# Retention queries and keys with features on the partitions, and a front with host-ordered transfers

## The chip, the cores and the metric

The kernel runs on one core of a Trainium2 chip. Its time is the device time of one execution in microseconds; the median of several runs counts, and beside it stands one profiled execution, from which all rows are taken.

## The reference, cut to what matters

A model of four layers over 256 latent tokens and 256 context tokens of 1024 features, in float32. The change touches the first layer, a retention mixer, and the way in which all weights are read. Cut to that:

```python
# modulation: silu(c) @ ada_w + ada_b -> shift, scale, ... (6 chunks of 1024)
def modulate(x, shift, scale):
    return rms_norm(x) * (1.0 + scale) + shift

# retention_mixer, 4 heads, q and k of 256, v of 512 features per head
q, k, v, g = split(h @ w_in)              # for latents and for context
k = k * RET_DK ** -0.5
ql, kl = rope_2d(ql), rope_2d(kl)         # only the latents are rotated
att = einsum('bihd,bjhd->bhij', q, k) * decay_mask
o = einsum('bhij,bjhv->bihv', att, v)     # latents see latents and context
y = (group_norm(o) * norm_g * silu(g)) @ w_out
```

`rope_2d` takes the 256 features of a head in two halves of 128, one by the token's row and one by its column; in each, feature i is rotated with feature i + 64.

## The kernel before

Everything is written out by hand, one instruction queue for each engine, with semaphores between them. Weights pass in units of 128 x 2048 floats (1 MB). SyncE's queue (SP) loads them in order of use into three raw slots, each unit with two transfers of 512 KB (L394), and waits for a slot until VectorE has made the low part of the unit that lay in it. ScalarE makes the high part of a unit (`w_hi`, a copy to the fp32r format, L609), VectorE the low part (`w_lo`, the difference, L1241). Activations are kept in two parts as well (`hT_hi`, `hT_lo`, cast L1371 and subtraction L1246; 8 k-tiles of 128 features x 512 tokens, of which 256 are latents and 256 context). A product is three matmuls: high by high, high by low, low by high (L2326, L2327, L2321 with the activations standing in the array; L2336, L2337, L2340 with the weights standing). `ahead(name)` on ScalarE and VectorE splits all units up to two behind the named one.

The front: `x` and `ctx` are normed (squares and root on ScalarE, product on VectorE, L1282), turned on TensorE (`x_turned`, L2269) and copied out of PSUM by ScalarE (L658). Meanwhile the modulation's first four chunks of 512 columns (2 MB each, in `FRONT_IN`) are multiplied on TensorE (`chunk`, `sums`, L2283), the sums copied as rows by VectorE (`row`, L1323), turned into columns (`to_cols`) and added up (`mod_cols`, L1331 and L1333). With shift and scale known for four k-tiles, ScalarE modulates (`modulate`, L630) and VectorE splits (`rows_split`). TensorE's queue takes latents and context apart: units `qa0` and `qb0` (queries and keys of head 0, k-tiles 0 to 3 and 4 to 7) are multiplied for token tiles 0 and 1 first, then for 2 and 3. The small vectors come as rows and are turned on TensorE (`cols_full`). `awake` multiplies zeros while TensorE would have nothing to do. The decay of the heads is a short series on VectorE (`decay_start`, `series`, `decay_end`), with one exponential on ScalarE between.

A head has six units: `qa`, `qb`, `g0`, `g1`, `va`, `vb`. `strip` makes queries and keys with tokens on the partitions; ScalarE copies them to `QK` (keys scaled, L705, L706), VectorE rotates (L1464 to L1468, semaphore `roped`), TensorE turns them with 16 transposes (L2269), ScalarE copies them to `QKT` (L720), and the score matmuls (L2457) read that. Between the transposes and the scores TensorE does the first k-tile of `vb`; behind the scores, the other three. VectorE multiplies the scores with the mask (L1487). Into the heads VectorE also weighs the later chunks of the modulation (`weigh`, L1361 and L1363), whose pieces of 1 MB GpSimd's queue (POOL) loads (L537), each as soon as the buffer is read. Head 0 begins on VectorE with the mask's arguments (L1433, L1434) after a wait for two transfers of constants; ScalarE's mask exponentials (L697 to L700) come ahead of its high part of `g00`.

Of the kernel before, what the change touches and what calls it, by code (L numbers as in the profile page):

```python
# [15 lines left out]
ALU = mybir.AluOpType  # L16
# [3 lines left out]
P = 128  # L20
# [29 lines left out]
C_ALL = C_MB + 768  # L50
# [62 lines left out]
FRONT = (0, 2, 1, 3)  # L113
# [66 lines left out]
def build(nc, A, out):  # L180
    ctx = ExitStack()
    with ctx:
        at_byte = [16512]

        def sb(name, shape, dt=F32, word=None):
            o = at_byte[0] if word is None else word
            n = 4 * math.prod(shape[1:])
            if word is None:
# [36 lines left out]
        names = ["unit_used", "hi_ready", "lo_ready", "out_stored", "const_in", "vec_in", "x_in", "x2_in", "dec_in",  # L225
# [3 lines left out]
                 "rstd_ready", "on_hi", "on_lo", "ident_in", "sz_set", "cols_full", "cols_read", "c_in",  # L229
                 "xt_full", "xt_read", "xm_ready", "h_part", "front_used", "xc_in", "ada_used", "row_ready", "at_full",  # L230
                 "mod_ready", "qk_read", "g_read", "qkt_full", "qkt_read", "sc_full", "sc_read", "v_read",
# [41 lines left out]
        vec, vec2, vec_c, lvec = at(8192, 128), at(8320, 128), at(8448, 128), const[:, C_DIST:C_DIST + 256]  # L273
# [51 lines left out]
        QK, PT, QKT, ON = at(0, 4, 512), at(0, 6, 256), at(2048, 4, 512), at(2048, 4, 512)  # L325
        VN, GT, ROPE = at(4096, 4, 512), at(6144, 4, 512), at(9728, 256)
# [55 lines left out]
        def _(sp):  # L382
            s = Side()

            def load(view, n, part):

                u = s.loaded
                assert n == SIZES[u], (u, n, SIZES[u])
                r = RAW_OF[u]
                v = RAW_BEFORE[u]  # L390
                if v is not None:
                    sp.wait_ge(sem["lo_ready"], v + 1)
                for j in range(2):
                    sp.dma_start(view(raw[:, r, 0:n], j), part(j)).then_inc(unit_in[r], 16)  # L394
                s.loaded += 1

            def by_k(w, k0, nk, c0, n):

                b = [0, nk // 2, nk]
                load(lambda d, j: d.rearrange("p (k n) -> p k n", k=nk)[:, b[j]:b[j + 1], :], nk * n,  # L400
                     lambda j: kpn(w)[:, k0 + b[j]:k0 + b[j + 1], c0:c0 + n])

            def pair(w, c0, gap):

                load(lambda d, j: d.rearrange("p (k g n) -> p k g n", k=KD, g=2)[:, :, j, :], UNIT,
                     lambda j: kpn(w)[:, :, c0 + j * gap:c0 + j * gap + P])

            def part(w, k0, c0, gap):

                load(lambda d, j: d.rearrange("p (k g n) -> p k g n", k=4, g=2)[:, :, j, :], UNIT,  # L410
                     lambda j: kpn(w)[:, k0:k0 + 4, c0 + j * gap:c0 + j * gap + 256])
# [2833 lines left out]
```

## Time and profile before

| | |
|---|---|
| median of 3 runs | 2022.6 us (2022.3 to 2022.95) |
| the profiled execution | span 2020.7 us, which is 1.9 us below that median |
| TensorE busy | 1988.9 us, 98% |
| VectorE, ScalarE, GpSimd busy | 1322.7, 857.5, 68.4 us |
| granted TensorE clock, mean | 0.997 |
| read from memory | 316.48 MB, 157 GB/s over the span |

The span runs from the first to the last instruction of the profiled execution. A busy engine is one that has an instruction in it; TensorE's are pipelined, so its true pace is the distance from one start to the next.

### The profile page before, as it was taken

The numbers are of one execution on the slowest core, as the hardware profiler recorded it, in microseconds if no ns is written. First come the engines' busy times: TensorE is split into PE (matmuls) and PEld (weight loads), VectorE is DVE, ScalarE is ACT, GpSimd is POOL, SyncE is SP. The second block draws the span as 40 slices with busy tenths as digits, with TensorE's granted clock in tenths as the row PEclk, the third lists the DMA queues.
The fourth block names the chain that finished last, engine by engine and source line by source line (L and its number), as shares of the span: only waits on it lengthen the run. The fifth ranks groups of instructions, "written<-read, shape, count | busy, mean of one in ns | idle before, by whom it ended". The sixth has DMA issues, their size and how long they took to land.

```text
span 2020.7 us, 25508 instructions
## 1 busy us (share of the span) xinstructions
PE 1988.9 (98%) x10263; PEld 1654.0 (82%) x10263; DVE 1322.7 (65%) x1642; ACT 857.5 (42%) x1007; POOL 68.4 (3%) x121
## 2 busy tenths in 40 slices
PE   8999999999999999999999999999999999999998
PEld 5878778778888888877778888899888888988887
DVE  5886979556555354576776565766866577678565
ACT  5332332224322222446665554554544356445442
POOL 0000000010111000000000000000000000000000
PEclk9999999999999999999999999999999999999999
DMA  9544444252554343332137555545655554546552
GB/s 357 184 151 136 144 148 145 84 167 74 172 155 158 104 151 126 102 113 84 53 103 219 168 177 177 188 165 170 216 194 193 176 172 162 196 157 218 189 190 81
DMA packets 250759, 319.19 MB, mean 158 GB/s; under 512 B 10113, under 2 KB 166066, under 8 KB 250130
## 3 DMA queue, kind: packets, MB, share of 16 engines
q1 hardware_dynamic: 235152, 262.77, 40.2%
q0 software_dynamic: 14416, 53.14, 7.8%
q8 instruction: 81, 1.33, 0.3%
q10 hardware_dynamic: 1074, 1.66, 0.2%
q14 instruction: 36, 0.29, 0.1%
HBM read 316.48 MB, written 1.05 MB: 157 GB/s over the span
## 4 chain that ended last, share of the span: by engine, by line
PE 86%; DVE 6%; ACT 2%; DVEq 2%; DMA 1%; issue 1%; ACTq 1%; SPq 0%
PE ps L2326 14%; PE ps L2327 14%; PE ps L2321 8%; PE ps L2881 6%; PE ps L3142 6%; PE ps L2340 5%; PE ps L2336 5%; PE ps L2337 5%; PE ps L2798 3%; PE ps L2269 3%; PE ps L3145 3%; PE ps L2406 2%; PE ps L2887 2%; PE ps L2891 2%; PE ps L2888 2%; PE ps L2801 2%
## 5 line engine op out<-in xcount | busy, mean ns | idle before, releaser
L1241 DVE TENSOR_TENSOR w_lo<-raw,w_hi 128x2048 fp32r<-128x2048 f32 (+1 forms) x244 | 553.0, 2271 | 239.1 <-ACT w_hi L609 238.3
L609 ACT ACTIVATE w_hi<-raw 128x2048 fp32r<-128x2048 f32 (+1 forms) x244 | 462.0, 1897 | 254.3 <-PE ps L2321 149.6
L2326 PE MATMUL ps<-w_hi,big_hi 128*128 128x512 f32 x760 | 298.8, 393 | 0.9 <-DVE big_lo L1739 0.7
L2327 PE MATMUL ps<-w_hi,big_lo 128*128 128x512 f32 x760 | 296.2, 390 | 0.0
L2336 PE MATMUL ps<-hT_hi,w_hi 128*128 128x512 f32 (+1 forms) x512 | 192.4, 380 | 1.9 <-issue 1.0
L2337 PE MATMUL ps<-hT_lo,w_hi 128*128 128x512 f32 (+1 forms) x512 | 190.3, 376 | 0.0
L2326 PE MATMUL ps<-w_hi,hT_hi 128*128 128x512 f32 x416 | 167.7, 403 | 4.6 <-DVE hT_lo L1246 4.6
L2326 PEld LDWEIGHTS ps<-w_hi,big_hi 128*128 128x128 f32 x760 | 142.8, 188 | 30.4 <-issue 1.0
L2327 PEld LDWEIGHTS ps<-w_hi,big_lo 128*128 128x128 f32 x760 | 142.9, 188 | 28.9 <-issue 0.5
L2327 PE MATMUL ps<-w_hi,hT_lo 128*128 128x512 f32 x416 | 163.2, 392 | 0.0
L3142 PE MATMUL ps<-h_both,w_hi 128*128 128x512 f32 x512 | 128.0, 392 | 0.0
L1363 DVE SCALAR_TENSOR_TENSOR raw<-front,const,raw 128x512 f32<-128x512 f32 x168 | 118.8, 748 | 7.0 <-issue 1.3
L2340 PE MATMUL ps<-hT_hi,w_lo 128*128 128x512 f32 (+1 forms) x512 | 119.8, 376 | 0.6 <-DVE w_lo L1241 0.6
L2326 PE MATMUL ps<-w_hi,h_both 128*128 128x512 f32 (+1 forms) x288 | 110.9, 388 | 3.2 <-DVE h_both L1246 3.2
L2336 PEld LDWEIGHTS ps<-hT_hi,w_hi 128*128 128x128 f32 x512 | 96.4, 188 | 20.3 <-issue 1.7
L2337 PEld LDWEIGHTS ps<-hT_lo,w_hi 128*128 128x128 f32 x512 | 96.5, 188 | 17.1 <-issue 0.2
L2327 PE MATMUL ps<-w_hi,h_both 128*128 128x512 f32 (+1 forms) x288 | 108.5, 380 | 0.0
L2321 PE MATMUL ps<-w_lo,big_hi 128*128 128x512 f32 x424 | 108.4, 390 | 0.0
L2321 PE MATMUL ps<-w_lo,hT_hi 128*128 128x512 f32 x416 | 108.2, 392 | 0.0
L2340 PEld LDWEIGHTS ps<-hT_hi,w_lo 128*128 128x128 f32 x512 | 92.3, 188 | 18.2 <-DVE w_lo L1241 0.8
L3142 PEld LDWEIGHTS ps<-h_both,w_hi 128*128 128x128 f32 x512 | 92.8, 189 | 17.1
L2326 PEld LDWEIGHTS ps<-w_hi,hT_hi 128*128 128x128 f32 x416 | 78.8, 189 | 25.7 <-issue 5.3
(314 smaller groups left out, 3027.4 us busy)
## 6 DMA issues: line engine op xcount, KB each, us to landing
raw<-ffn_w_in SPq DMA_DIRECT2D x88, 512.0 KB, 5.1
raw<-w_in SPq DMA_DIRECT2D x80, 512.0 KB, 4.6
raw<-w_up SPq DMA_DIRECT2D x64, 512.0 KB, 4.7
raw<-w_down SPq DMA_DIRECT2D x64, 512.0 KB, 4.5
raw<-ret_w_in SPq DMA_DIRECT2D x48, 512.0 KB, 5.4
front<-ada_w POOLq DMA_DIRECT2D x24, 1024.0 KB, 5.5
raw<-ffn_w_out SPq DMA_DIRECT2D x40, 512.0 KB, 4.5
raw<-ada_w POOLq DMA_DIRECT2D x64, 256.0 KB, 4.3
```

The lines of the kernel that those rows point to most:

```text
L609: act.activation(SPLIT_HI[PAIR_OF[u]][:, 0:m], raw[:, RAW_OF[u], 0:m], ACT.Copy).then_inc(sem["hi_ready"], 1)
L1241: op(SPLIT_LO[PAIR_OF[u]][:, 0:m], raw[:, RAW_OF[u], 0:m], SPLIT_HI[PAIR_OF[u]][:, 0:m].bitcast(F32), ALU.subtract).then_inc(sem["lo_ready ...
L1363: i = stt(out=acc[:, m, :], in0=rows[:, x, :], scalar=SZ[:, k, m:m + 1], in1=acc[:, m, :], op0=ALU.mult, op1=ALU.add)
L2269: return pe.transpose(out, src, ident[0:src.shape[0], 0:src.shape[0]])
L2321: i = pe.matmul(bank(b + t), x(k0 + k)[0][:, t * P:(t + 1) * P], w[1][:, k, :], start=False, stop=last and k == nk - 1)
L2326: pe.matmul(out, x[0][:, t * P:(t + 1) * P], w, start=start, stop=False)
L2327: pe.matmul(out, x[1][:, t * P:(t + 1) * P], w, start=False, stop=False)
L2336: pe.matmul(out, w[0][:, k, js], hT(k)[0][:, c:c + n], start=(k == 0), stop=False)
L2337: pe.matmul(out, w[0][:, k, js], hT(k)[1][:, c:c + n], start=False, stop=False)
L2340: i = pe.matmul(out, w[1][:, k, js], hT(k)[0][:, c:c + n], start=False, stop=(k == KD - 1))
L2881: i = pe.matmul(dst, x(k0 + k)[0][:, t * P:(t + 1) * P], w[1][:, k, :], start=False, stop=stop and k == nk - 1)
L3142: pe.matmul(out, w[0][:, k, js], h2_both[:, :, k, :], start=(k == 0), stop=False)
```

## The change

Queries and keys of all heads are made with features on the partitions: `features` takes the weights as the standing and the activations as the moving operand, as `feature` did for the gates. ScalarE copies the latents' queries and keys to `QKL` and those of the context straight to `QKT`. VectorE rotates the latents from `QKL` into `QKT`; the partner of a feature lies 64 partitions away, so the product with the sine is written across (`SWAP`). The 16 transposes, their PSUM copy and the semaphores `qkt_full` and `qkt_read` are gone; `roped` is now waited for behind the first k-tile of `vb`. The keys' scale is applied with the mask. The cosines and sines lie with features on the partitions; those of the column half are a third transfer of constants (`ROT_COS[1]`), queued on POOL behind `mod_ready` 4 and ahead of the pieces of the later modulation.

All weights come in one array in order of use, each unit with 8 KB in a row for each partition, in one transfer. The modulation's chunks are stored likewise; chunk j of the first four now holds 256 columns of shift and 256 of scale, so each serves two k-tiles. The small vectors come as columns, with no turning. `x` and `ctx` are loaded first, then `qa0`, chunks 0 to 2, `qb0`, chunk 3. In the front latents and context go together: `first_high` and `first_low` multiply one k-tile for all 512 tokens, as soon as VectorE has it (`modulated`, which takes ScalarE's part as well); ScalarE copies the rows instead of VectorE.

```diff
@@ SP
-                for j in range(2):
-                    sp.dma_start(view(raw[:, r, 0:n], j), part(j)).then_inc(unit_in[r], 16)
+                    sp.dma_start(raw[:, r, 0:m], A["units"][u, :, 0:m]).then_inc(unit_in[r], 16)
             def modulation(j):
+                for h in range(2):
+                    sp.dma_start(FRONT_IN[2 * j + h], A["ada"][j, :, 4 * h:4 * h + 4, :]).then_inc(front_in[2 * j + h], 16)
             sp.dma_start(X4[:, 0:2, :], token_rows(A["x"][0])).then_inc(sem["x_in"], 16)
+            sp.dma_start(X4[:, 2:4, :], token_rows(A["ctx"][0])).then_inc(sem["xc_in"], 16)
+            load(FIRST_END["qa0"])
             modulation(0)
+            modulation(1)
             modulation(2)
+            load(FIRST_END["qb0"])
             modulation(3)
+            load(TOTAL_UNITS)
@@ POOL
-            pool.wait_ge(front_in[3], 32)
-            fetch(X4[:, 2:4, :], token_rows(A["ctx"][0]), sem["xc_in"])
-            pool.wait_ge(sem["front_used"], 2)
+            pool.wait_ge(sem["front_used"], 1)
             fetch(dec[:, 0, :], bcast(A["ret_decay_logit"].rearrange("a b c -> a (b c)"), 8), sem["dec_in"])
...
             pool.wait_ge(sem["front_used"], 4)
             fetch(const[:, C_DIST:C_SZ], A["table"][:, C_DIST:C_SZ], sem["const_in"])
             fetch(const[:, C_RS:C_SEL], A["table"][:, C_RS:C_SEL], sem["const_in"])
+            pool.wait_ge(sem["mod_ready"], 4)
+            fetch(ROT_COS[1], A["table"][:, C_RK:C_RK + 256], sem["const_in"])
@@ ACT
+            first_squares(0)
+            first_root(0)
+            first_squares(1)
+            first_root(1)
+            for t in range(4):
+                turned_x(t)
             split(FIRST_END["qa0"])
+            row(0, 8960, 1)
+            row(1, 9472, 2)
             act.wait_ge(sem["dec_abs"], s.next("dec_abs"))
             act.activation(dec[:, 2, :], dec[:, 1, :], ACT.Exp, scale=-1.0).then_inc(sem["dec_exp"], 1)
+            row(0, 8960, 3)
             split(FIRST_END["qb0"])
+            row(1, 9472, 4)
...
-                    act.wait_ge(sem["const_in"], 32)
+                    act.wait_ge(sem["const_in"], 48)
...
-                act.activation(QK[:, :, 0:256], ps[:, a:a + 4, 0:256], ACT.Copy)
-                act.activation(QK[:, :, 256:512], ps[:, a:a + 4, 256:512], ACT.Copy, scale=RDK ** -0.5).then_inc(sem["qk_read"], 1)
+                act.activation(QKL, ps[:, a:a + 4, 0:256], ACT.Copy)
+                act.activation(QKT[:, :, 256:512], ps[:, a:a + 4, 256:512], ACT.Copy).then_inc(sem["qk_read"], 1)
...
-                act.wait_ge(sem["qkt_full"], h + 1)
-                act.activation(QKT[:, :, :], ps[:, b:b + 4, :], ACT.Copy).then_inc(sem["qkt_read"], 1)
@@ DVE
+            def modulated(c):
+                xm = at(4096 + 512 * c, 2, 256)
+                for m, x in enumerate((XTL, XTC)):
+                    ts(xm[:, m, :], x[:, c, :], mod[:, 0, 8 + c, m:m + 1], mod[:, 0, c, m:m + 1], ALU.mult, ALU.add)
+                drain()
+                dve.tensor_copy(hT_hi[:, c, :], at(4096 + 512 * c, 512))
+                drain()
+                lo(hT_lo[:, c, :], at(4096 + 512 * c, 512), hT_hi[:, c, :]).then_inc(sem["h_part"], 1)
+            first_norm(0)
+            first_norm(1)
+            dve.wait_ge(sem["xt_read"], 4)
+            mod_cols(2, 0)
+            modulated(0)
+            modulated(1)
             split(FIRST_END["qa0"])
+            mod_cols(3, 1)
+            modulated(2)
+            modulated(3)
@@
+            mod_cols(2, 2)
+            modulated(4)
+            modulated(5)
+            split(FIRST_END["qb0"])
             decay_start()
             series(15, 13, 11, 9)
+            mod_cols(3, 3)
+            modulated(6)
+            modulated(7)
             decay_end()
@@ DVE, in a head
+                for n in range(2):
+                    x = QKL.rearrange("p (g n) t -> p g n t", n=2)[:, :, n, :]
+                    y = QKT.rearrange("p (g n) t -> p g n t", n=2)[:, :, n, 0:256]
+                    sn = ROT_SIN[n].unsqueeze(1).to_broadcast([P, 2, 256])
+                    for r in (0, 64):
+                        op(SWAP[64 - r:P - r], x[r:r + 64], sn[r:r + 64], ALU.mult)
+                    op(y, x, ROT_COS[n].unsqueeze(1).to_broadcast([P, 2, 256]), ALU.mult)
+                    drain()
+                    i = op(y, y, SWAP, ALU.add)
...
-                    i = op(PT[:, t, :], sc[:, t, :], g, ALU.mult)
+                    i = stt(out=PT[:, t, :], in0=sc[:, t, :], scalar=RDK ** -0.5, in1=g, op0=ALU.mult, op1=ALU.mult)
@@ PE
+            pe.wait_ge(sem["ones_set"], 1)
+            awake(24)
+            pe.wait_ge(sem["ident_in"], 16)
             x_turned(0)
             x_turned(1)
+            awake(8)
             x_turned(2)
             x_turned(3)
+            pe.wait_ge(sem["silu_c"], 1)
+            chunk(0, 0)
+            awake(4)
+            to_cols(2, 8960)
+            awake(8)
+            first_high("qa0", 0)
+            first_high("qa0", 1)
+            chunk(1, 1)
+            first_low("qa0", 0)
+            to_cols(3, 9472)
+            first_low("qa0", 1)
             chunk(2, 0)
+            first_high("qa0", 2)
+            to_cols(2, 8960)
+            first_high("qa0", 3)
+            first_low("qa0", 2)
+            used(first_low("qa0", 3))
             chunk(3, 1)
+            first_high("qb0", 4)
             to_cols(3, 9472)
+            first_high("qb0", 5)
+            first_low("qb0", 4)
+            first_low("qb0", 5)
+            first_high("qb0", 6)
+            first_high("qb0", 7)
+            first_low("qb0", 6)
+            used(first_low("qb0", 7))
@@ PE, in a head
-                    used(strip(a, f"qa{h}", hT, 0, 4, range(4), True, False))
+                    used(features(a, f"qa{h}", 0, range(4), 0, 512, True))
...
+                strip(a, f"vb{h}", hT, 4, 4, (0,), False, False)
+                mod_read()
                 pe.wait_ge(sem["roped"], h + 1)
-                mod_read()
-                for c in range(4):
-                    for t in range(4):
-                        i = turn(bank(b + c)[:, t * P:(t + 1) * P], QK[:, t, c * P:(c + 1) * P])
-                i.then_inc(sem["qkt_full"], 1)
-                strip(a, f"vb{h}", hT, 4, 4, (0,), False, False)
-                pe.wait_ge(sem["qkt_read"], h + 1)
```

## Rows read from the trace of the kernel before

**Rows 1.** The page: the span, and each engine's busy time.

```profile
span 2020.7 us, 25508 instructions
...
PE 1988.9 (98%) x10263; PEld 1654.0 (82%) x10263; DVE 1322.7 (65%) x1642; ACT 857.5 (42%) x1007; POOL 68.4 (3%) x121
```

**Rows 2.** TensorE's waits: us in total, times, longest.

```profile
PE ps L2326 <- DVE hT_lo L1246: 4.6, 1, 4.6
```

**Rows 3.** Windows of stretches: length, busy by engine, granted clock, DMA, GB/s.

```profile
0.00:56.06 56.06, 48.56 (x243) 34.43 (x243) 30.66 (x72) 28.95 (x42) 4.91 (x12) 0.94 0.94 332
20.30:24.90 4.60, 0.02 (x1) 0.00 (x0) 1.49 (x5) 3.98 (x5) 0.00 (x0) 0.84 1.04 403
24.95:30.20 5.25, 5.25 (x12) 4.08 (x13) 4.82 (x8) 3.65 (x6) 0.00 (x0) 0.50 1.05 384
56.06:95.23 39.17, 39.17 (x190) 32.84 (x189) 34.26 (x52) 13.22 (x10) 2.25 (x4) 1.00 0.60 199
95.23:390.00 294.77, 293.92 (x1303) 231.11 (x1302) 231.70 (x346) 88.61 (x68) 14.05 (x18) 1.00 0.42 140
```

**Rows 4.** Timeline of TensorE: start us, us, engine, instruction.

```profile
18.78 0.66 PE L2269 MATMUL ps<-const,arena 128*128 128x128 f32 x4
...
34.88 3.64 PE L2283 MATMUL ps<-front,const 128*32 128x512 f32 x32
...
56.06 0.19 PEld L2336 LDWEIGHTS ps<-hT_hi,w_hi 128*128 128x128 f32 x1
...
95.23 2.10 PE L2457 MATMUL ps<-arena 128*128 128x256 f32 x9
```

**Rows 5.** The chain that ended last, front and head 1: start us, us, what.

```profile
49.19 1.81 PE ps L2321 x8
...
178.51 1.75 PE ps L2269 x16
```

**Rows 6.** Timeline of VectorE, front and head 0.

```profile
23.70 0.43 DVE L1371 CAST hT_hi<-arena 128x512 fp32r<-128x512 f32 x1 [2.91 <-ACT arena L630]
24.20 0.69 DVE L1246 TENSOR_TENSOR hT_lo<-arena,hT_hi 128x512 fp32r<-128x512 f32 x1
24.81 0.42 DVE L1371 CAST hT_hi<-arena 128x512 fp32r<-128x512 f32 x1
...
39.52 0.19 DVE L1331 TENSOR_REDUCE mod<-ps 128x8 f32<-128x32 f32 x1
...
49.12 0.36 DVE L1433 TENSOR_SCALAR arena<-const 128x384 f32<-128x384 f32 x1
...
82.77 0.48 DVE L1464 TENSOR_TENSOR arena<-arena,const 128x128 f32<-128x128 f32 x2
...
88.89 1.22 DVE L1343 TENSOR_REDUCE mod<-ps 128x8 f32<-128x1024 f32 x1
...
90.26 2.29 DVE L1241 TENSOR_TENSOR w_lo<-raw,w_hi 128x2048 fp32r<-128x2048 f32 x1
```

**Rows 7.** Windows of transfers, the last column in GB/s.

```profile
22.00:24.00 2.00, 0.00 (x0) 0.00 (x0) 0.30 (x1) 1.92 (x4) 0.00 (x0) 0.86 1.09 432
34.00:40.00 6.00, 5.70 (x46) 2.36 (x45) 3.71 (x8) 4.63 (x6) 1.15 (x3) 1.00 1.10 349
```

**Rows 8.** Timeline of ScalarE, front and head 0.

```profile
7.74 1.05 ACT L651 ACTIVATE arena<-arena 128x1024 f32<-128x1024 f32 x1
...
14.16 1.94 ACT L658 ACTIVATE arena<-ps 128x1024 f32<-128x1024 f32 x2 [2.67 <-PE ps L2269]
...
52.02 1.90 ACT L609 ACTIVATE w_hi<-raw 128x2048 fp32r<-128x2048 f32 x1
...
92.69 1.88 ACT L720 ACTIVATE arena<-ps 128x2048 f32<-128x2048 f32 x1 [10.73 <-PE ps L2269]
```

**Rows 9.** POOL's transfers: to landing, 45 to 400 us, then 38 to 48.

```profile
DMA to landing us min/median/max: 5.4/5.5/5.8
...
DMA to landing us min/median/max: 4.9/7.3/10.3
```

More of the change, by code:

```diff
@@ L49 @@
 C_MB = C_MA + 512
-C_ALL = C_MB + 768
+C_RK = C_MB + 768
+C_ALL = C_RK + 256
 C_HELD = C_DC
@@ L403, in pair @@
[L403 to L411, printed above, removed]
-            sp.dma_start(const[:, 0:P], A["table"][:, 0:P]).then_inc(sem["ident_in"], 16)
@@ L2355, in _, with features @@
-            pe.wait_ge(sem["vec_in"], 96)
-            turn(bank(7)[:, 0:P], vec[:, :])
-            turn(bank(7)[:, P:P + 33], vec2[0:33, :]).then_inc(sem["cols_full"], 1)
+            def features(b, name, k0, ks, c, n, first):
+                w = unit(name, 4)
+                for k in ks:
+                    for j in range(4):
+                        out, js = bank(b + j)[:, c:c + n], slice(j * P, (j + 1) * P)
+                        pe.matmul(out, w[0][:, k, js], hT(k0 + k)[0][:, c:c + n], start=first and k == 0, stop=False)
+                        pe.matmul(out, w[0][:, k, js], hT(k0 + k)[1][:, c:c + n], start=False, stop=False)
+                lows(name)
+                for k in ks:
+                    for j in range(4):
+                        i = pe.matmul(bank(b + j)[:, c:c + n], w[1][:, k, j * P:(j + 1) * P], hT(k0 + k)[0][:, c:c + n],
+                                      start=False, stop=k0 + k == KD - 1 and c + n == 512)
+                return i
@@ L2363, in x_turned, with first_high @@
                 i.then_inc(sem["xt_full"], 1)
[L2365 to L2371 removed]
+            def first_high(name, k):
+                w = unit(name, 4)
+                pe.wait_ge(sem["h_part"], k + 1)
+                for j in range(4):
+                    out, js = bank(4 + j), slice(j * P, (j + 1) * P)
+                    pe.matmul(out, w[0][:, k % 4, js], hT(k)[0], start=(k == 0), stop=False)
+                    pe.matmul(out, w[0][:, k % 4, js], hT(k)[1], start=False, stop=False)
@@ L2372, in _, with first_low @@
+            def first_low(name, k):
+                w = unit(name, 4)
+                lows(name)
+                for j in range(4):
+                    i = pe.matmul(bank(4 + j), w[1][:, k % 4, j * P:(j + 1) * P], hT(k)[0], start=False, stop=(k == KD - 1))
+                return i
+            pe.wait_ge(sem["ones_set"], 1)
+            awake(24)
+            pe.wait_ge(sem["ident_in"], 16)
             x_turned(0)
             x_turned(1)
-            half(0, 0, 1).then_inc(sem["front_used"], 1)
```

412 lines of the change are left out of this document (170 added, 242 removed).

## The prediction

> **What bounds the kernel now.** I read the head of the page first: TensorE is busy for 1988.9 of 2020.7 us, VectorE for 1322.7, ScalarE for 857.5 [rows 1]. So I looked for TensorE's idle time. The longest of its waits is 4.6 us in the front, for VectorE's first low part of the activations [rows 2]; the windows put 7.5 of its 31.8 idle us ahead of 56.06 us and less than one between there and 390 us, so in the retention heads TensorE never stands still [rows 3]. Head 0's first gate matmul starts at 56.06 us, its scores at 95.23 [rows 4]. The same view shows the clock: in the gap from 20.3 to 24.9 us TensorE does nothing, and behind it, from 24.95 to 30.2 us, the granted clock is 0.50, the 1.2 GHz level. Last I looked at what else must be on time: VectorE works 34.3 of the 39.2 us of head 0 ahead of its scores [rows 3], so it is nearly full there and not in the later heads, where it has 231 of 295 us. Two kinds of change can therefore pay: fewer TensorE instructions, and a shorter front. The profiled execution is 2020.7 us long, 1.9 below the median of the runs; I make the sum on the execution and carry the difference over.
>
> **TensorE work removed in the heads.** Each head turns queries and keys with 16 transposes. In head 1 the chain gives the 16 of them 1.75 us [rows 5]. The projections of the new form have as many matmuls of the same shape, 96 of 128x512, at 0.227 us from start to start (eight in 1.81 us [rows 5]), so nothing changes there. The score matmuls are the same 24. In heads 1 to 3 VectorE and ScalarE are timed from TensorE's own progress (the high and low parts wait for units that TensorE has finished), the rotation ends some 20 us ahead of its reader, and the low part of the second value unit is done before it is wanted; nothing there can take the place of the transposes. Gain: 3 x 1.75 = 5.25 us. Head 0 is another matter, below.
>
> **ScalarE and VectorE in the heads.** ScalarE loses one copy of 2048 elements from PSUM per head, 1.88 us, which TensorE covered with one k-step of the value projection. The scale of the keys goes into the six score products, in scalar_tensor_tensor form; I take no cost for it, since it stays one pass over the same elements (the bound from above is a few tenths, under 9 us of TensorE's value matmuls). The rotation goes from 6.1 us (82.77 to 88.89 [rows 6]) to eight instructions of 512 elements. One such costs 0.61 us (two instructions of 512 elements, cast and subtraction, take 1.11 from cast to cast, 0.50 of it the cast with its drain [rows 6]); with the drains 2 x 2.6 = 5.2 us, 0.9 less. A half-width instruction on 64 partitions isn't in this trace; I price it by its length along the row, and the bounds are 0.3 and 0.75 us each, so the rotation has 4.0 to 5.8 us.
>
> The rows show nothing of instructions that change their partitions. The Trainium skill (VectorE: DVE Perf Modes, Two Vector instructions with no wait between them) says that an instruction whose operands start in another quadrant than those before is held until all earlier ones have finished. By that rule six instructions of a rotation would each pay about what a drain costs here, and the gain in head 0 would be 0.5 us smaller, 2016.1 instead of the time below; no run here shows it yet.
>
> **The host-ordered transfers.** A unit becomes one transfer of 1 MB with 8 KB rows instead of two of 512 KB with rows of 0.5 to 2 KB. TensorE waits for no weight transfer after the front, so beyond it I count nothing: the cover is three slots ahead of use. In the front the rate is 349 GB/s where 1 KB rows of the projection weights dominate (34 to 40 us) and 432 where the context with its 8 KB rows runs (22 to 24 us) [rows 7]. The front needs 12.6 MB up to its last modulation chunk, and the first x tiles come first: at 385 GB/s the first chunk is whole at 17.2 us, the others at 22.5, 27.9 and 36.3. At 430 GB/s they come 1.5 to 4 us earlier.
>
> **The front, step by step.** The front ended at 56.06 us. Now I lay the new order out with the durations of before. x lands near 6 us (ScalarE took it up at 7.74 only because it had turned the vectors first [rows 8]); two squares, table load, root and first product: TensorE can turn token tile 0 at 10.6. It turns tiles 1 to 3 by 16.0, each pair held up by ScalarE's copies out of PSUM (0.97 each [rows 8]). Chunk 0 takes TensorE 1.8 us (32 records in 3.64 us are two chunks [rows 4]) and is done at 18.05; but ScalarE has its copy of the row queued behind the fourth x copy and the high part of unit qa0 (1.9 us), so the row is there at 19.6. Turning it 0.7 (the row at 18.78 [rows 4]), the columns' sums on VectorE 0.75 (an estimate: two small reduces of 0.19 [rows 6], two additions like them, one drain): 21.0. A k-tile then takes VectorE two modulating instructions, cast and subtraction: 0.5 + 1.1 = 1.6 us. TensorE needs 8 x 0.227 = 1.8 us for its high products. So k-tiles 0 and 1 are ready at 22.6 and 24.2, TensorE has them done at 26.3, chunk 1 at 28.0, the lows and the turned row by 30.4, chunk 2 at 32.2. VectorE has k-tiles 2 and 3 at 31.9 and 33.5, and only then the first decay instruction, for which ScalarE waits before it copies the third row: 34.5, a small new wait. From there TensorE has no gap: k-tile 3 and two lows 38.9, chunk 3 40.6, k-tile 4, the turned row, k-tile 5 and their lows 46.7, the rest 52.2. VectorE, meanwhile: columns 2 and k-tiles 4, 5 at 39.2, low part of qb0 41.5, decay series 43.7, columns 3, k-tiles 6, 7 at 47.7, end of the decay 49.3. That is 3.9 us better on TensorE (2.5 of it because no 4.6 us gap brings the clock down: 12 matmuls at 0.43 instead of 0.23 us) and 0.2 us worse on VectorE, whose front ended at 49.12 [rows 6].
>
> **What is late next.** Head 0 hangs on VectorE and ScalarE. ScalarE's mask exponentials and then the high part of g00 (start 52.02, 2.9 us behind VectorE's start at 49.12 [rows 6, 8]) give 54.1, so TensorE stands still from 52.2 to 54.1. VectorE weighs a 1 MB piece of the later modulation before it makes g00's low part. That piece is now queued on POOL behind the last cosines, and those behind the fourth chunk's columns at 44.5: with 5.5 us from issue to landing [rows 9] it lands near 50.7, 0.7 us after VectorE wants it. VectorE's chain from its start to the low part of unit vb0 took 49.12 to 92.55 (start 90.26, 2.29 long [rows 6]), 43.4 us. Now: 49.3 + 0.7 + 43.4 - 0.9 = 92.5; four low matmuls, and the scores start at 93.4 instead of 95.23 [rows 4]. TensorE alone would be there at 54.1 + 39.2 - 1.7 = 91.6. So the transposes of head 0 are not earned: what they covered was that low part. Gain of front and head 0: 1.8 us. The third transfer of constants, issued at 44.6, must land before 49.3; nothing of its size is in the rows, the 1 MB ones take 5.5 us, so it can cost at most 0.8.
>
> Sum: 1.8 + 5.25 = 7.0 us; 2020.7 - 7.0 = 2013.7 us of span, or 2022.6 - 7.0 = 2015.6 us. The bounds: with VectorE not in the way (faster landing, cheap rotation, shorter front) TensorE's own line is 52.2 + 39.2 - 1.7 = 89.7, 5.5 us for front and head 0, total 10.8, 2011.8 us. Against it, POOL transfers that take the longest landing of this trace's busy stretch, 10.3 us [rows 9], cost another 5, total 2.0, 2020.6 us.
>
> **Rivals.** (a) Head 0 hides nothing: VectorE's front is shorter than I add up and TensorE is the bound throughout, gains of 9 to 12 us, 2010.6 to 2013.6. For it: the new front has no long idle stretch and 8 KB rows land faster. Against it: VectorE has 34.3 us of work in 39.2 already. (b) The front gives back what the heads bring: the third constant and the first piece land late, or the clock falls in the gaps ahead of 22.6 us and the first 24 products run at 0.43 (24 x 0.2 = 4.8 us). Gains of 0 to 5, 2017.6 to 2022.6. For it: landings of up to 10.3 us; the clock did fall behind 4.6 us of nothing. Against it: my longest gap is under 2 us. (c) Slower: the four chunks of the front become four round trips in a row. TensorE sums, ScalarE copies, TensorE turns, VectorE sums and modulates two k-tiles, TensorE multiplies: 1.7 + 0.6 + 0.7 + 0.75 + 3.2 + 3.6 + 1.8 = 12.3 us each if nothing overlaps, from 16.0 to 65.4 against 56.06: 9.3 us lost, 5.25 gained, 2026.7. It turns the sign once each trip loses 2.3 us of overlap. Before, ScalarE modulated and rows were copied by VectorE, so trips overlapped on two engines; now VectorE does all of it. Against it: the order of TensorE's queue puts each chunk ahead of the products of the one before. (d) The edit of the transfers moves the whole kernel: 12 us or more. Nothing speaks for it: no weight transfer is among TensorE's waits.
>
> **Chances.** Forecast, a gain of 5 to 9 us: 0.53. (a) 0.15, (b) 0.22, (c) 0.07, (d) 0.03. The bound for telling apart is 0.2%, 4.0 us, so 2018.6 divides: a quarter of (b) lies below it. Faster 0.53 + 0.15 + 0.05 + 0.03 = 0.76, same 0.18, slower 0.06 (the mild end of (c) counts as same). The range from 2011.0 to 2020.5 holds the forecast, nearly all of (a) and three quarters of (b), some 0.83; the likeliest case's own range is 2013.6 to 2017.6.
>
> **What would show it.** After: TensorE's first gate matmul at 54 us with a wait of some 2 us for ScalarE's high part; a wait for the low part of g00 below 1 us and for that of vb0 of 1 to 2 us; scores of head 0 at 93.4; the granted clock at full from 10 to 50 us; heads 1 to 3 each 1.75 us shorter; rotation 5.2 us; VectorE's mask arguments at 49.3. Wrong it would be if chunk 3's columns came much after 44.5, if VectorE found the piece landed later than 51, or if a wait for the rotation appeared in heads 1 to 3.

## The result and the profile after

The changed kernel takes 2025.38 us (median of 20 runs, 2024.24 to 2027.81), the kernel before 2022.51 (20 runs, 2021.58 to 2023.34): a ratio of 1.0016, 95% interval 1.0009 to 1.0022. It is slower by 2.9 us where I forecast 7.0 us faster; by the bound of 0.2% that is no change, though the interval lies above 1, and it lies outside the range. The profiled execution is 2024.0 us long.

The page, against [rows 1]:

```profile
span 2024.0 us, 25190 instructions
...
PE 1985.3 (98%) x10252; PEld 1650.5 (82%) x10252; DVE 1327.2 (66%) x1629; ACT 844.1 (42%) x991; POOL 63.2 (3%) x121
```

TensorE is busy for 3.6 us less than before, and yet the span is 3.3 us longer: work went away, and 6.9 us of idle time came (38.7 us against 31.8). TensorE's waits, against [rows 2], say where (total, times, longest):

```profile
PE ps L2153 <- DVE arena L1158: 7.4, 1, 7.4
...
PE ps L2220 <- ACT w_hi L494: 2.7, 1, 2.7
...
PE ps L2205 <- DVE w_lo L1120: 1.4, 1, 1.4
...
PE ps L2260 <- DVE hT_lo L1125: 1.1, 1, 1.1
```

The old 4.6 us wait is gone. A 7.4 us wait stands ahead of the very first transposes instead, on VectorE's normalized tokens, and 2.7 us ahead of head 0's first gate product. The timelines of TensorE and then of VectorE, against [rows 4, 6] (start, us, engine, instruction, idle before):

```profile
15.68 3.65 PE L2153 MATMUL ps<-const,arena 128*128 128x128 f32 x16 [7.40 <-DVE arena L1158]
19.12 3.12 PE L2245 MATMUL ps<-ones 128*128 128x128 f32 x16
22.08 1.91 PE L2153 MATMUL ps<-const,arena 128*128 128x128 f32 x16
23.92 0.64 PE L2167 MATMUL ps<-front,const 128*32 128x512 f32 x4
...
64.69 0.50 PE L2220 MATMUL ps<-hT_hi,w_hi 128*128 128x512 f32 x1 [2.67 <-ACT w_hi L494]
```

```profile
13.87 0.18 DVE L1147 TENSOR_SCALAR cols<-cols 128x32 f32<-128x32 f32 x1 [12.73 <-DMA cols<-columns]
...
28.86 0.74 DVE L1255 TENSOR_SCALAR arena<-arena,mod 128x256 f32<-128x256 f32 x2
29.67 0.43 DVE L1257 CAST hT_hi<-arena 128x512 fp32r<-128x512 f32 x1
30.17 0.69 DVE L1125 TENSOR_TENSOR hT_lo<-arena,hT_hi 128x512 fp32r<-128x512 f32 x1
30.78 0.73 DVE L1255 TENSOR_SCALAR arena<-arena,mod 128x256 f32<-128x256 f32 x2
...
59.85 0.36 DVE L1319 TENSOR_SCALAR arena<-const 128x384 f32<-128x384 f32 x1
...
94.84 1.39 DVE L1349 TENSOR_TENSOR arena<-arena,const 64x512 f32<-64x512 f32 x2
96.24 0.69 DVE L1350 TENSOR_TENSOR arena<-arena,const 128x512 f32<-128x512 f32 x1
...
100.56 1.22 DVE L1219 TENSOR_REDUCE mod<-ps 128x8 f32<-128x1024 f32 x1
```

What to see: VectorE does nothing until 13.87 us, because the first thing in its queue after a memset is to add one to columns that come by a transfer. The normalization of the tokens, whose squares were done at 8.1 us, is queued behind it. In the kernel before, the column work stood ahead of the normalization too, and there it could start at 10.22 us: it is the late landing that is new. Then 16 transposes take 3.65 us, and the same 16, three microseconds later, 1.91. The windows show why (length, busy by engine, granted clock, DMA share, GB/s), against [rows 3]:

```profile
12.00:20.00 8.00, 4.32 (x21) 4.35 (x22) 3.73 (x11) 4.15 (x8) 0.00 (x0) 0.50 1.02 420
...
59.85:66.00 6.15, 3.48 (x16) 2.55 (x15) 4.78 (x9) 5.40 (x7) 0.00 (x0) 1.00 0.46 193
66.00:70.00 4.00, 4.00 (x12) 3.13 (x11) 3.84 (x4) 3.73 (x3) 0.53 (x1) 0.58 0.37 88
70.00:105.33 35.33, 33.92 (x158) 27.89 (x158) 33.67 (x44) 7.57 (x5) 1.58 (x3) 1.00 0.58 201
105.33:390.00 284.67, 283.81 (x1244) 223.81 (x1243) 229.25 (x322) 81.43 (x64) 10.19 (x18) 1.00 0.42 144
```

The granted clock is at the 1.2 GHz level behind the 7.4 us gap (0.50 from 12 to 20 us), and from 66 to 70 us, behind the 2.7 us gap, it is 0.58, most of the window at that level. The scores of head 0 start at 105.33 us instead of 95.23, 10.1 us late. From there heads 1 to 3 run as forecast. The starts of the score products, read from the timelines of the two kernels, and in the runs below:

| kernel | mask arguments | scores h0 | h1 | h2 | h3 | span |
|---|---|---|---|---|---|---|
| before | 49.12 | 95.23 | 182.86 | 270.50 | 358.13 | 2020.7 |
| after | 59.85 | 105.33 | 191.22 | 277.10 | 362.98 | 2024.0 |
| e2_heads_only | 48.46 | 93.73 | 179.60 | 265.47 | 351.33 | 2013.6 |
| e3_units_only | 49.67 | 95.75 | 183.39 | 271.01 | 358.69 | 2020.5 |
| e1_cols_later | 53.76 | 98.69 | 184.57 | 270.49 | 356.34 | 2017.6 |
| e6_small_first | 55.21 | 100.50 | 186.37 | 272.24 | 358.10 | 2019.4 |
| e12_short_rows | 52.82 | 98.89 | 186.43 | 272.29 | 358.16 | 2019.2 |
| e7_awake_longer | 52.09 | 97.00 | 184.44 | 270.31 | 356.19 | 2017.3 |
| e8_both_modulate | 51.96 | 97.67 | 183.57 | 269.44 | 355.35 | 2016.8 |
| e13_all | 50.30 | 95.77 | 183.75 | 269.61 | 355.46 | 2017.0 |
| e16_scores_first | 50.66 | 92.04 | 178.93 | 264.80 | 350.67 | 2012.2 |
| e14_heads_units | 49.91 | 94.70 | 180.56 | 266.42 | 352.29 | 2013.7 |

From head to head it is 87.63 us before and 85.88 after: 1.75 us each.

### The profile page after: what moved, and what is told of

Same layout as the page of the kernel before. It is cut to its first block, busy times and chain, and to the rows that moved or that the text cites. A ratio compares the mean times of both kernels' runs of the same rounds, so it can differ in the third digit from the quotient of the medians.

```text
span 2024.0 us, 25190 instructions
## 1 busy us (share of the span) xinstructions
PE 1985.3 (98%) x10252; PEld 1650.5 (82%) x10252; DVE 1327.2 (66%) x1629; ACT 844.1 (42%) x991; POOL 63.2 (3%) x121
## 4 chain that ended last, share of the span: by engine, by line
PE 84%; DVE 8%; DVEq 4%; ACT 2%; issue 1%; DMA 1%; ACTq 1%; POOL 0%
PE ps L2210 12%; PE ps L2211 12%; PE ps L2205 6%; PE ps L2783 6%; PE ps L3044 6%; PE ps L2224 5%; PE ps L2220 5%; PE ps L2221 5%; PE ps L2700 3%; PE ps L2153 3%; PE ps L3047 3%; PE ps L2313 2%; PE ps L2789 2%; PE ps L2793 2%; PE ps L2790 2%; PE ps L2703 2%
## 5 line engine op out<-in xcount | busy, mean ns | idle before, releaser
L2210 PE MATMUL ps<-w_hi,hT_hi 128*128 128x512 f32 x288 | 114.9, 399 | 0.0
L2211 PE MATMUL ps<-w_hi,hT_lo 128*128 128x512 f32 x288 | 112.3, 390 | 0.0
L2205 PEld LDWEIGHTS ps<-w_lo,big_hi 128*128 128x128 f32 x424 | 79.5, 188 | 16.9 <-DVE w_lo L1120 0.3
L2153 PE MATMUL ps<-const,arena 128*128 128x128 f32 x564 | 73.9, 279 | 13.8 <-DVE arena L1158 7.4
```

The lines of the kernel that those rows point to most:

```text
L2153: return pe.transpose(out, src, ident[0:src.shape[0], 0:src.shape[0]])
L2205: i = pe.matmul(bank(b + t), x(k0 + k)[0][:, t * P:(t + 1) * P], w[1][:, k, :], start=False, stop=last and k == nk - 1)
L2210: pe.matmul(out, x[0][:, t * P:(t + 1) * P], w, start=start, stop=False)
L2211: pe.matmul(out, x[1][:, t * P:(t + 1) * P], w, start=False, stop=False)
```

## The experiments

Each was run with the kernel before on the same chip; the ratio is to that one. The first two ask which part of the change is to blame.

**The features in the heads, on the old front** (the kernel before with these parts of the diff; the third transfer of constants and the two sets of sines come with them, and head 0's products in the front take the new form too).

```diff
-                    used(strip(a, f"qa{h}", hT, 0, 4, range(4), True, False))
+                    used(features(a, f"qa{h}", 0, range(4), 0, 512, True))
...
-                for c in range(4):
-                    for t in range(4):
-                        i = turn(bank(b + c)[:, t * P:(t + 1) * P], QK[:, t, c * P:(c + 1) * P])
-                i.then_inc(sem["qkt_full"], 1)
```

> The kernel before, with the queries and keys of all heads with features on the partitions (no transposes, rotation across the partitions, third transfer of constants) and nothing else: transfers and front as before. Theory A (the heads bring what the transposes cost, the front lost it): heads 1 to 3 each 1.75 us shorter, head 0 between 0 and 1.75, the front 0 to 1 later for the constants: 2017.0 us (2015.5 to 2018.5). Rival C (the heads give nothing, since VectorE's chain sets them): 2021.5 to 2024.

2016.37 us (2015.40 to 2016.86), ratio 0.9968 (0.9956 to 0.9981): 6.2 us faster than before. Heads 1 to 3 bring the 5.25 us that were forecast. Head 0's scores start 1.5 us earlier (93.73 against 95.23), which is nearly what its transposes cost. The forecast had them not earned, since they covered vb0's low part; on the old front that part is done at 92.1 us, 0.7 ahead of its products, and TensorE has no wait in head 0.

**The host-ordered weight units alone, on the old front and heads.**

```diff
-                for j in range(2):
-                    sp.dma_start(view(raw[:, r, 0:n], j), part(j)).then_inc(unit_in[r], 16)
+                    sp.dma_start(raw[:, r, 0:m], A["units"][u, :, 0:m]).then_inc(unit_in[r], 16)
```

> The kernel before, with only the weight units taken from one array in order of use, 8 KB rows, one transfer per unit; modulation, small vectors, front and heads as before. Theory A (TensorE waits for no weights): 2022.5 us within 1.0. Rival D (the long rows speed the whole kernel or slow it): more than 2 us away on either side.

2022.31 us (2021.25 to 2022.58), ratio 0.9998 (0.9989 to 1.0007). Neutral, as laid out: no weight transfer was among TensorE's waits. So the loss is in what the front does, which the last run below, with both parts together, confirms: against the first run, which has the old front, the changed kernel's head 0 scores are 11.6 us late.

**VectorE's column work later.** The changed kernel, with the wait for the small vectors and three instructions moved behind the second normalization.

```diff
-            dve.wait_ge(sem["vec_in"], 32)
-            ones_in = ...
             first_norm(0)
             first_norm(1)
+            dve.wait_ge(sem["vec_in"], 32)
+            ones_in = ...
```

> The changed kernel, with VectorE's wait for the small vectors and the three column instructions put behind both norms. Theory A (the front is late because VectorE waits until 13.87 us for two small transfers that it does not need for the norm; TensorE then stands still for 7.4 us and its clock falls): the root is at about 9.5 instead of 14.5 us, the clock stays up, the first gate matmul comes about 8 us earlier (56.5 instead of 64.7), and the time is 2017.4 us (2015.5 to 2018.5), 8 less than the changed kernel's 2025.4. Rival B (the wait is absorbed, the four round trips of the modulation set the front): at most 2 us less, 2023.4 or more.

2019.43 us (2017.50 to 2022.47), ratio 0.9988 (0.9979 to 0.9997): 6.0 us less than the changed kernel where 8 were expected. The eleven times spread over 5 us, six from 2017.50 to 2019.43 and five from 2021.85 to 2022.47, so this median is less firm than the others; the profiled execution belongs to the first six. TensorE's timeline of this run:

```profile
10.66 3.05 PE L2154 MATMUL ps<-const,arena 128*128 128x128 f32 x16 [2.40 <-DVE arena L1153]
13.51 2.53 PE L2246 MATMUL ps<-ones 128*128 128x128 f32 x16
15.88 1.91 PE L2154 MATMUL ps<-const,arena 128*128 128x128 f32 x16
```

The first transposes start at 10.66; the prediction's chain had 10.6. But a gap of 2.40 us is left, and behind it 16 transposes take 3.05 us, so the tiles are turned at 17.7, not at 16.0.

**The small vectors first.** Why are 24.5 KB late by 11.7 us? In the changed kernel the transfers up to 16 us are these (KB each, us from issue to landing):

```profile
front<-ada SPq DMA_DIRECT2D x8, 1024.0 KB, 18.4
...
arena<-x SPq DMA_DIRECT2D x1, 1024.0 KB, 4.9
...
const<-table ACTq DMA_DIRECT2D x1, 64.0 KB, 7.3
cols<-columns ACTq DMA_DIRECT2D x1, 48.0 KB, 9.5
cols<-columns ACTq DMA_DIRECT2D x1, 24.5 KB, 11.7
cols<-columns ACTq DMA_DIRECT2D x1, 8.0 KB, 5.1
```

They go by ScalarE's queue, SP's queue is full of 1 MB transfers at the same time, and the later a small one was issued, the later it landed after it. The edit moves the four small ones to SP's queue, ahead of x.

```diff
-            act.dma_start(cols[:, V_C:V_NG], A["columns"][:, V_C:V_NG]).then_inc(sem["c_in"], 16)
+            sp.dma_start(cols[:, V_C:V_NG], A["columns"][:, V_C:V_NG]).then_inc(sem["c_in"], 16)
...
             sp.dma_start(X4[:, 0:2, :], token_rows(A["x"][0])).then_inc(sem["x_in"], 16)
```

> The changed kernel, with the four small transfers issued on the queue of SP ahead of x instead of on ScalarE's. Theory A2 (they are late because they share the transfer engines with 3 MB and more of long rows queued by SP): they land by about 5 us, x some 1 us later than before, the front is 7 us earlier and the time 2018.5 us (2016.5 to 2019.5). Rival (they are slow by themselves, 128 rows of 196 to 384 bytes): they land near 12 us again and the time stays within 1.5 of 2025.4.

2021.92 us (2020.48 to 2023.63), ratio 0.9997 (0.9989 to 1.0006), 3.5 us less than the changed kernel, half of what was expected. Now they land 1.8 to 2.3 us after their issue:

```profile
4.42 0.18 DVE L1147 TENSOR_SCALAR cols<-cols 128x32 f32<-128x32 f32 x1 [3.29 <-DMA cols<-columns]
...
9.84 0.17 DVE L1153 TENSOR_SCALAR st<-st 128x2 f32<-128x2 f32 x1 [5.09 <-ACT arena L529]
```

But x stands behind them: VectorE has the sums of its squares at 9.84 instead of 8.25 (the run before), TensorE's gap becomes 3.6 us, and its first 16 transposes take 3.52.

**Short rows.** The other way to get them earlier: the first transfers of SP (x, the context, the first two units, the four chunks) as four transfers each, with rows of 2 KB instead of 8; the same bytes, the same order.

```diff
-                    sp.dma_start(FRONT_IN[2 * j + h], A["ada"][j, :, 4 * h:4 * h + 4, :]).then_inc(front_in[2 * j + h], 16)
+                    for k in range(4):
+                        sp.dma_start(FRONT_IN[2 * j + h][:, k, :], A["ada"][j, :, 4 * h + k, :]).then_inc(front_in[2 * j + h], 16)
```

> The changed kernel, with x, context, the first two units and the first four chunks as four transfers of 2 KB rows each instead of one of 8 KB rows; the small vectors are issued by ScalarE as before. If the small transfers are late because each of SP's rows of 8 KB goes in one piece ahead of theirs on the shared engines, they land by 9 us and the first root comes 4 to 5 us earlier, with a time of 2018 to 2021 us. If they are late for the sheer bytes that share the engines, or for their own 128 short rows, they land at 12 to 14 us again and the time stays at 2024 to 2027.

2021.08 us, ratio 0.9991 (0.9982 to 1.0001), 4.3 us less than the changed kernel. Nine of its ten times lie from 2018.78 to 2022.67; the tenth is 4031.19 us, and nothing here explains it. The same view, and VectorE's timeline:

```profile
const<-table ACTq DMA_DIRECT2D x1, 64.0 KB, 4.1
cols<-columns ACTq DMA_DIRECT2D x1, 48.0 KB, 4.6
cols<-columns ACTq DMA_DIRECT2D x1, 24.5 KB, 4.9
cols<-columns ACTq DMA_DIRECT2D x1, 8.0 KB, 3.6
```

```profile
7.03 0.18 DVE L1154 TENSOR_SCALAR cols<-cols 128x32 f32<-128x32 f32 x1 [5.89 <-DMA cols<-columns]
```

The last small transfer lands 4.9 us after its issue instead of 11.7, with the issue order of ScalarE's queue untouched. So it is the length of the rows on the other queue, with the division into more transfers that goes with it, that held them up; the two were not tried apart. Fewer bytes ran beside them, too (225 and 350 GB/s from 2 to 4 and 4 to 6 us, against 301 and 404), but that is 13 to 25% less, and the landing takes less than half the time. The Trainium skill (DMA: Bandwidth & Descriptors, Queues, rings and completion order) says that each DMA engine takes turns between the queues it has work for, a packet at a time. The trace agrees in its sign: up to 16 us SP's queue moves 5.51 MB in 752 packets in the changed kernel and 4.71 MB in 2574 here, so a packet of the other queue is 7.3 KB against 1.8, and a small transfer that waits for such turns lands after 11.7 us against 4.9. The turns themselves are not seen in a trace. In the kernel before, only x (1 MB) had rows of 8 KB beside the small vectors; the chunks had rows of 2 KB.

**TensorE kept busy up to the first transposes.** The kernel of the column run, with 35 products of ones instead of 24 ahead of them.

```diff
-            awake(24)
+            awake(35)
             pe.wait_ge(sem["ident_in"], 16)
```

> The kernel with the column work behind the norms (2019.4 us), and 35 instead of 24 products of ones ahead of the first transposes, so that TensorE has no gap of 2.4 us there. Theory E (the gap brings the clock to 1.2 GHz from about 11.5 to 14.5 us, so 16 transposes take 3.05 instead of 1.9 us and the eight products behind them 2.53 instead of 2.0): the clock stays at 1.00, tiles 2 and 3 are turned at 14.1 instead of 15.9, head 0 starts 1.8 us earlier: 2017.6 us. Rival (the clock falls anyway, or the copies on ScalarE set the pace): within 0.7 of 2019.4.

```profile
5.79 4.96 PE L2246 MATMUL ps<-ones 128*128 128x128 f32 x43
10.64 1.94 PE L2154 MATMUL ps<-const,arena 128*128 128x128 f32 x16
12.42 1.95 PE L2246 MATMUL ps<-ones 128*128 128x128 f32 x16
14.20 1.91 PE L2154 MATMUL ps<-const,arena 128*128 128x128 f32 x16
```

No gap, 1.94 us for 16 transposes, all tiles turned at 16.04 (the prediction had 16.0), and the mask arguments and head 0's scores are 1.7 us earlier than in the column run. And yet the time is 2019.31 us (2018.29 to 2019.51), ratio 0.9983 (0.9975 to 0.9992), the same as without: the table shows that head 1's scores start 0.1 us earlier, so in the profiled executions the 1.7 us are lost inside head 0. I come back to that below.

**The modulation divided between two engines.** The column run, with the latents' half of each k-tile modulated by ScalarE.

```diff
-                for m, x in enumerate((XTL, XTC)):
-                    ts(xm[:, m, :], x[:, c, :], mod[:, 0, 8 + c, m:m + 1], mod[:, 0, c, m:m + 1], ALU.mult, ALU.add)
+                ts(xm[:, 1, :], XTC[:, c, :], mod[:, 0, 8 + c, 1:2], mod[:, 0, c, 1:2], ALU.mult, ALU.add)
                 drain()
+                dve.wait_ge(sem["xm_ready"], s.next("xm_ready"))
```

> The kernel with the column work behind the norms, and ScalarE modulating the latents of each k-tile while VectorE modulates the context (it did both). Theory F (VectorE's chain sets head 0, and a k-tile takes it 1.92 us instead of the 1.6 of the forecast): a k-tile takes 1.5 us, VectorE reaches the mask's arguments some 3 us earlier (53.8 to 50.8), the scores of head 0 start 2.5 to 3 us earlier, 2016.6 us. Rival (the round trips by TensorE and ScalarE's copies set the front, and ScalarE's share comes late): within 1 of 2019.4.

2018.42 us (2017.07 to 2020.25), ratio 0.9979 (0.9970 to 0.9989). A k-tile takes VectorE 1.6 us instead of 1.92, the mask arguments come 1.8 us earlier, head 0's scores 1.0, and the median is 1.0 lower, where 2.8 were expected. Between the two VectorE loses 0.8 us: it waits 1.02 us for the first piece of the later modulation instead of 0.61, and stands still for 0.43 us within the rotation. TensorE waits 2.4 us for the low part of unit vb0, and here the clock stays up behind the wait:

```profile
96.62 1.21 PE L2216 MATMUL ps<-w_lo,hT_hi 128*128 128x512 f32 x4 [2.42 <-DVE w_lo L1130]
```

**All three, and g00 ahead of the mask.** Column work, 35 products, ScalarE's modulation, and both parts of unit g00 split ahead of the mask's exponentials and of the first weighing.

```diff
+                if h == 0:
+                    split(FIRST_END["g00"])
                 act.wait_ge(sem["mask_arg"], h + 1)
```

> All together: column work behind the norms, the longer stretch of products of ones, both engines modulating, and in head 0 the high and low parts of unit g00 ahead of the mask's exponentials and of the first weighed piece. If E and F hold and add up, 2014.7 us (2013.5 to 2016.5), with no wait of TensorE above 1 us between 20 and 100 us; if head 0's VectorE chain is all that counts, the last edit adds nothing and the time is 2015 to 2016.5.

2017.96 us (2015.65 to 2018.94), ratio 0.9978 (0.9969 to 0.9987), 3.3 more than expected, and with two waits of TensorE above 1 us in head 0 where none was expected (1.5 for the low part of a gate unit, 2.9 for that of vb0). Scores of head 0 start 3 us earlier than in the column run, those of head 1 only 0.8. TensorE's timeline and windows in head 0:

```profile
93.90 2.08 PE L2220 MATMUL ps<-w_lo,hT_hi 128*128 128x512 f32 x4 [2.92 <-DVE w_lo L1132]
95.77 7.43 PE L2374 MATMUL ps<-arena 128*128 128x256 f32 x24
```

```profile
94.00:98.00 4.00, 4.00 (x10) 3.19 (x11) 2.23 (x1) 0.00 (x0) 0.00 (x0) 0.50 0.74 260
98.00:102.00 4.00, 4.00 (x16) 3.35 (x15) 0.00 (x0) 0.00 (x0) 0.00 (x0) 0.75 0.65 264
```

That is where the front's gain goes. VectorE is full in head 0, so TensorE reaches vb0's low part only when VectorE has made it. That moment itself comes earlier by what VectorE gained, 3.8 us against the column run (93.90 against 97.66); what is lost again is lost behind the wait. There the granted clock is at the 1.2 GHz level: from the first low product to the scores it is 1.9 us instead of 1.0, and the 24 score products take 7.2 instead of 5.2. The run with 35 products has the same: the low products start 1.8 us earlier than in the column run, behind a wait of 2.1 us, the granted clock is 0.84 and 0.74 in the two windows after it, and the chain has 6.7 us of scores.

```profile
95.84 1.37 PE L2206 MATMUL ps<-w_lo,hT_hi 128*128 128x512 f32 x4 [2.08 <-DVE w_lo L1120]
```

The run before this one is the comparison that tells the wait from the clock: its wait, 2.42 us, is longer than that with 35 products, its clock stays at 1.00 from 96 to 104 us, and it keeps the whole 1.0 us by which its low part came earlier. From the first low product to the end of the scores it takes 6.05 us there, 6.0 in the column run, 7.7 in the run with 35 products and 8.95 in this one. So the clock costs 1.7 and 2.9 us, and the wait for a full VectorE costs only the gains that TensorE made alone.

**The scores ahead of vb0's low part.** The score products need VectorE's rotation and its sum of the modulation, but not the low part that VectorE makes next.

```diff
-                strip(a, f"vb{h}", hT, 4, 4, (0,), False, False)
+                if h:
+                    strip(a, f"vb{h}", hT, 4, 4, (0,), False, False)
+                else:
+                    w = unit("vb0", 4)
+                    for t in range(4):
+                        high(bank(a + t), hT(4), t, w[0][:, 0, :], False)
                 mod_read()
                 pe.wait_ge(sem["roped"], h + 1)
...
+                if h == 0:
+                    lows("vb0")
+                    for t in range(4):
+                        pe.matmul(bank(a + t), hT(4)[0][:, t * P:(t + 1) * P], w[1][:, 0, :], start=False, stop=False)
```

> This is the kernel of the run e13_all (column work behind the second norm, 35 products ahead of the first transposes, the latents modulated by ScalarE, the gate's first unit split ahead of the mask) with one thing more: in head 0 the 24 score products stand ahead of the four low products of the value unit vb0's first k-step, so that they no longer stand behind VectorE's low part of vb0. Theory: a front that is 2 to 4 us shorter has been paid back in head 0, because VectorE is full there: TensorE waits 2.9 us for vb0's low part, and behind that wait the granted clock is at its lower level (24 score products in 7.2 us instead of 5.2). If so, the scores start when VectorE has added up the modulation, at about 91.7 us (95.8 in e13_all) and take 5.2 to 5.5 us, head 1's scores start near 178.4 (183.8), and the execution has about 2011.6 us, 5.4 less than e13_all; the median is then 2012.5 to 2014. Rival: the wait is moved and not removed (TensorE waits as long for the sum of the modulation, and the clock falls all the same): then head 1's scores start at 182 or later and the time stays within 1.5 us of e13_all's 2018.

```profile
92.04 5.45 PE L2379 MATMUL ps<-arena 128*128 128x256 f32 x24 [0.71 <-DVE mod L1228]
97.14 1.28 PE L2384 MATMUL ps<-w_lo,hT_hi 128*128 128x512 f32 x4
```

2013.96 us (2013.51 to 2014.54), ratio 0.9959 (0.9947 to 0.9971): 4.0 us less than the kernel it is made from, 11.4 less than the changed kernel, and 8.1 less than the one before on the same chip. (The run it is made from was on another chip; each against the kernel before on its own chip, the difference is 3.5.) A 2.9 us wait became one of 0.7, the windows have the clock at 1.00 throughout, and head 1's scores start 4.8 us earlier, at 178.93 instead of 183.75; 2.9 of that are what the low clock had cost. It is the fastest version of this study.

**Heads and units on the old front.** The first two runs together.

> The kernel before with the features in the heads and with the weight units as one host-ordered transfer each; the front, its transfers and its modulation stay as they were. Theory: the two parts do not touch each other, so the sum is that of the features alone: 2016.4 us (2015.4 to 2016.9), with the first scores near 93.7 and head 1's at 179.6. Rival: with fewer packets on SP's queue the units come earlier and VectorE, which is full in head 0, has fewer gaps: up to 1 us less. Other side: the transfers of 8 KB rows delay a small transfer in the front, which would show as first scores at 94.5 or later and 1 us more.

2015.74 us (2015.55 to 2016.62), ratio 0.9969 (0.9957 to 0.9981). Within the spread of the first run, and 9.6 us below the changed kernel: by so much the new front is worse than the old one. With the five edits of the run above it is 1.8 us better; whether the old front would gain as much from the order of the scores was not tried. Head 0's scores are 1.0 us later than in the first run, and from head 3's scores to the end it takes 1661.4 us instead of 1662.3: the units cost a little in the front and bring about as much later.

## Why the prediction was wrong

**The step that failed** is the start of the front: "two squares, table load, root and first product: TensorE can turn token tile 0 at 10.6". It counted what ScalarE and VectorE do to x, and left out what stands ahead of it in VectorE's queue: a wait for the small vectors. In the kernel it is in plain sight, since `dve.wait_ge(sem["vec_in"], 32)` comes ahead of `first_norm`, and I priced no landing for them: the second one landed 11.7 us after its issue, and VectorE began at 13.87. The run that moves the wait has its first transposes at 10.66. Of the 11.9 us between the forecast 93.4 and the measured 105.33 for head 0's scores, this is 5.1 (15.68 against 10.6).

**The clock** takes 2.8 more: all tiles are turned at 23.9, 7.9 us late, of which 5.1 are the start. I had the granted clock full from 10 to 50 us, because my longest gap was to be under 2 us; but the 24 products of ones end at 8.3, so my own chain had a gap of 2.3 us up to 10.6, and even with the transposes at 10.66 the gap is 2.40 us. The run with 35 products shows both, 3.05 against 1.94 us for the same transposes. Rival (b) had a falling clock, but on the first 24 products behind chunk 0 and at 4.8 us; it came on the first transposes and cost 2.8.

**A modulating pair** was taken at 0.5 us and takes 0.81 from its start to the cast (28.86 to 29.67): two instructions with two scalars per partition, 0.37 each from start to start, and a drain. So a k-tile is 1.92 us and not 1.6, eight of them 2.6 us more. The mask arguments are 10.55 us late: 7.9 and 2.65. That these 2.65 are the pair's is read from the rows; the run that divides the modulation brings 1.8 of them back.

**In head 0** the last 1.3 us: the rotation takes 5.7 us (94.84 to 100.56), 0.5 more than forecast, and from the mask arguments to it 35.0 instead of 34.3, of which 0.4 is the first piece of the later modulation: VectorE waits 1.13 us for it, and 0.7 were forecast. The rotation is where the Trainium skill's rule (VectorE: DVE Perf Modes, Two Vector instructions with no wait between them) and the rows were weighed. An instruction of 512 elements starts 0.70 us after the one before, where I had 0.61 without the rule; with it the sum was 5.7. The trace agrees with the rule. The half-width instructions on 64 partitions cost the same 0.70: the row's length sets the time, as priced.

**What held.** Heads 1 to 3 bring 1.75 us each, 5.25 together (from head 0's scores to head 3's 257.65 us against 262.90). The transfers are neutral. On the old front the heads give 6.2 us. The waits named for the new front are there, 2.7 us for g00's high part and 1.4 for vb0's low part, though all 10 us late. After head 3's scores the changed kernel is 1.6 us shorter (1661.0 against 1662.6), which none of my terms has; the two kernels with host-ordered units alone or with the heads have 0.8 and 1.2 of it, the heads alone 0.3, so half or more of it seems to come with the units. What the units change there was not looked into.

**The sum again, with what was measured:** 2013.7 + 5.1 + 2.8 + 2.65 + 1.35 - 1.6 = 2024.0 us of span, the profiled one. The terms are stretches of one trace against the forecast's, so they add up by themselves; the runs bear out the first two (6.6 us of head 0's scores back without the wait, 1.7 more without the gap). Rival (c), the round trips in a row, did not happen: the trips overlap as laid out, and removing the wait, the cold clock and the dear pair gives the forecast mask arguments within 1.0 us (50.30 against 49.3).

**And the range.** Its upper end, 2020.5, came from late POOL transfers. "VectorE works 34.3 of the 39.2 us" was right, and its consequence went further than I drew it. What TensorE alone gains in the front it waits for at vb0's low part, and where the clock falls behind that wait, part of what VectorE gained goes too: of 2.9 us at head 0's scores 0.8 is left at head 1's, and 1.5 in the median. With the order of TensorE's queue changed there, the forecast 2015.6 is beaten (2013.96), but by a kernel with five edits more than the one that was forecast.

## What to carry to other kernels

Read every wait that a change puts at the head of an engine's queue, and ask for each how late its transfer can be when another queue's long rows run beside it; then move the wait to its first reader. Price an idle stretch of TensorE by the work behind it as well: here gaps of 2.4 and 7.4 us ahead of the first transposes cost 1.7 and 2.8 us more in slower products, and waits of 2.1 and 2.9 us in head 0 cost 1.7 and 2.9. And where the next engine in line is full, what TensorE gains ahead of it is only a gain once TensorE has something to do that doesn't need that engine.

## What the runs showed that I had not expected

A transfer of 24.5 KB took 11.7 us to land beside 1 MB transfers with 8 KB rows on another queue, 4.9 beside the same bytes in 2 KB rows, and 2.3 when it stood ahead of them on their own queue. Gaps of much the same length had different consequences. Ahead of vb0's low part the granted clock fell to the 1.2 GHz level behind 2.08 us (35 products) and behind 2.02 us (short rows), and stayed at the 2.4 GHz level behind 2.42 us (divided modulation). Ahead of the first transposes it fell behind 2.40 us (the column run), and behind 2.06 us (short rows) the same 16 transposes took 1.94 us at the 2.4 GHz level:

```profile
11.46 1.94 PE L2160 MATMUL ps<-const,arena 128*128 128x128 f32 x16 [2.06 <-DVE arena L1165]
```

So these rows give no single length of a gap at which it falls, and what else decides stays open. It may also be what spreads the times of the column run over 5 us, but only one execution of it was profiled.
